# A hybrid decoder layer: low halves of the values in the ones' columns, and the probabilities added up on GpSimd

## The chip, the cores and the metric
The kernel runs on one core of a Trainium2 chip. The metric is the device time of one execution in microseconds. The core has a matrix engine (TensorE, PE in the profile), VectorE (DVE), ScalarE (ACT), GpSimd (POOL) and SyncE (SP), which issues nearly all DMAs. Each engine works through its own queue in order; semaphores join them.

## The reference
One layer of a decoder on x of 2048 tokens by 1024. After a normalisation, one projection feeds three token mixers side by side: a gated linear recurrence, forgetting attention with 6 heads of 64, and gated linear attention with 4 heads. Their outputs pass one projection and a residual, then a gated feed-forward layer of width 2816. The change is inside the forgetting attention, cut here to what matters:

```python
s = (jnp.einsum('bhqd,bhkd->bhqk', qb, k) * scale
     + cb[..., :, None] - cum[..., None, :])
s = jnp.where(k_pos[None, :] <= q_pos[:, None], s, -jnp.inf)
p = jax.nn.softmax(s, axis=-1)
return jnp.einsum('bhqk,bhkd->bhqd', p, v)
```

## The kernel before
All is float32. Matrix products are made of float32r operands: each value is split into a high half (a copy in float32r) and a low half (value minus high half), and a product is three: high x high, high x low, low x high (`split_products`, L77 to L79). The first function, `project_in_and_recur`, projects three of the four blocks of 512 tokens. The second, `mix_and_feed_forward`, projects the last block and runs everything else.

The second function is a row of 328 units on TensorE. A unit is one output tile of 128 x 512: 8 triples of products (6 in some), weights of 128 x 1024. Its kinds are p (projection), o (output projection), g and u (gate and up), d (down). For each unit SyncE loads the raw weights, ScalarE makes the high half `w_hi` (L1108), GpSimd the low half `w_lo` (L1093) as soon as the unit two before is done on TensorE, and VectorE reads the result out of PSUM.

The token mixers are woven into these units: `side` gives for each unit a list of turns, and TensorE does them between the triples of the unit, evenly spaced. All engines walk through the same list in the same order. Attention of block b is woven into units 14 to 22 (block 0), 61 to 89, 139 to 165 and 215 to 241. Its steps are, by letter:

- S: a piece of the scores, 128 queries by up to 512 keys (L1665, L1666; with the mask L1668), into one of two banks of `fa_s_ps`. VectorE takes its row maxima (L1383, `fa_ch_max`). A piece needs its bank free: `bank_free` waits for the reader of the use before the last.
- M: VectorE joins the maxima and splits them (L1388, cast L1393, L1395, `fa_m_cols`), TensorE turns them (L1675), ScalarE copies them into rows of the queries (L1146). The first T of the head waits for it.
- T: scores again, transposed, 128 keys by up to 512 queries, less the maximum (L1691, L1692). ScalarE makes of them `fa_probs` (exponentials in float32, L1141) and `fa_p_hi` (the same in float32r, L1142), VectorE the low half `fa_p_lo` (L1401). There are three buffers of each.
- V: the products with the values (`times_v`, L1707 to L1709) into `fa_o_ps`, two turns after the T of the same item. Values are loaded as 192 columns per key tile: high halves, ones, low halves.
- F: the end of a head (`finish`), issued in the turn of the second key tile of the next head.

An item is one head and one tile of 128 keys. A head of block b has 4(b+1) items; the last three have 384, 256 and 128 query columns, all others 512. Over 4 blocks and 6 heads that is 240 items and 24 heads. In a turn of block 1 to 3 stand one T, one V and one or two S; a unit carries 2 turns in block 1, 2 to 3 in block 2, 3 to 4 in block 3, and 3 in block 0.

Before, the three products of an item are these: high halves and ones (128 columns) times `p_hi`, low halves (64 columns) times `p_hi` into partitions 0 to 63, high halves and ones times `p_lo`. So partitions 0 to 63 of `fa_o_ps` hold the sum of probabilities times values and partitions 64 to 127 the sum of the probabilities, 64 times. `finish` is a reciprocal of the latter (L1408) and a product (L1412).

GpSimd runs, for each unit, the split of the weights, and now and then memsets: `value_ones(b)` (L1048) fills the ones into `fp_v_nat` at the head of each block's operand stage.

Of the kernel before, what the change touches and what calls it, by code (L numbers as in the profile page):

```python
# [14 lines left out]
F32 = mybir.dt.float32  # L15
F32R = mybir.dt.float32r
U32 = mybir.dt.uint32
ALU = mybir.AluOpType
# [538 lines left out]
def mix_and_feed_forward(nc, vec, mod, held, xT, w_in, w_gates, w_alpha, w_out, w_gate_up, w_down, consts, fox_rows, proj, mix, q_split, ka, kb, v_split, yT):  # L557
# [136 lines left out]
    bank_uses = lambda s: [s] if s[0] in ("S", "M", "mean") else [("gate0", s[1]), ("gate1", s[1])] if s[0] == "L" else {("X", 1): [("rows", s[1][0])], ("G", 0): [("z", s[1][:2])], ("G", 4): [("att0", s[1][:2]), ("att1", s[1][:2])],  # L694
# [46 lines left out]
    with ExitStack() as ctx:  # L741
# [20 lines left out]
        mean_ones, eps, scale_a = sb("ff_mean_ones", [P, P]), sb("ff_eps", [P, 1]), sb("ff_scale_a", [P, KD])  # L762
        ident, ident_r, masks_r = sb("fa_ident", [P, P]), sb("fa_ident_r", [P, P], F32R), sb("fa_masks_r", [P, 2, P], F32R)
# [8 lines left out]
        with region:  # L772
# [4 lines left out]
            v_nat = there("fp_v_nat", [P, 2, 2, TPB, 3 * HEAD_DIM], F32R)  # L777
# [9 lines left out]
        with region:  # L787
# [7 lines left out]
            inv_sum, o_t = there("fa_inv_sum", [HEAD_DIM, BLK]), there("fa_o_t", [P, 2, BLK])  # L795
# [7 lines left out]
        v_hi, v_ones, v_lo = (v_nat[:, :, :, :, i * HEAD_DIM:(i + 1) * HEAD_DIM] for i in range(3))  # L803
# [21 lines left out]
        m_turned, m_copied = sem("fa_m_turned"), sem("fa_m_copied")  # L825
        st_done, p_hi_done, p_lo_done, pv_done, inv_done, fin_done = sem("fa_st_done"), sem("fa_p_hi_done"), sem("fa_p_lo_done"), sem("fa_pv_done"), sem("fa_inv_done"), sem("fa_fin_done")
# [5 lines left out]
        v_t, v_hi_done, v_lo_done, ones_made = sem("fp_v_t"), sem("fp_v_hi_done"), sem("fp_v_lo_done"), sem("fp_ones_made")  # L832
# [45 lines left out]
        with nc.Block() as block:  # L878
# [156 lines left out]
            def _(pool):  # L1035
# [38 lines left out]
                def prepare(j):  # L1074
                    for b in range(NBLK):
                        if j >= GIVEN and j in (x_load[b], g_load[b], q_fill[b], fill_at[b]):
                            pool.wait_ge(lo_ready, split(j))
                        if j == x_load[b]:
                            value_ones(b)
# [867 lines left out]
```

## Time and profile before

| | |
|---|---|
| median of 3 runs | 2987.01 us (2985.84 to 2988.37) |
| the profiled execution | 2993.32 us, its span 2991.5 us |
| granted TensorE clock, mean | 0.973 |
| TensorE matmul busy | 2818.5 us, 94% of the span, 12416 instructions |
| VectorE busy | 1463.1 us, 49% |
| ScalarE busy | 1185.2 us, 40% |
| GpSimd busy | 1035.5 us, 35%, 488 instructions |
| DMA queue q1, share of 16 engines | 44.6% |

Busy time is the union of an engine's instructions. Matmuls overlap each other in the records (a record holds the time through the array as well), so what a matmul costs in a stream is read from one start to the next. In the rows below a name such as L1708 is a line of the kernel, and an entry in brackets behind an instruction is the time its engine stood idle before it, and what it waited for.

### The profile page before, as it was taken

The page shows a single profiled execution, that of the slowest core. Times are in us where ns is not written, and L with a number is a line of the kernel's source. Part 1 is how long each engine was busy: PE and PEld are TensorE (multiplying, and loading weights), DVE is VectorE, ACT ScalarE, POOL GpSimd, SP SyncE. Part 2 cuts the span into 40 slices and gives each one's busy share as a digit, 9 for nine tenths or more (in the row PEclk, how much of TensorE's full clock was granted, in tenths as well). Part 3 has the DMA queues.
Part 4 walks back from the last instruction along what each step waited for, and adds up shares of the span by engine and source line. Part 5 has one row for each costly group of instructions (what it writes and reads, how often), then busy time and mean ns, then how long its engine had stood idle before and what let it go on. Part 6 is the DMA issues. An engine that isn't in the chain of part 4 may idle for free.

```text
span 2991.5 us, 32965 instructions
## 1 busy us (share of the span) xinstructions
PE 2818.5 (94%) x12416; PEld 2211.5 (74%) x12416; DVE 1463.1 (49%) x1876; ACT 1185.2 (40%) x1654; POOL 1035.5 (35%) x488
## 2 busy tenths in 40 slices
PE   8998998788988999999999999999999999999999
PEld 4786876466757777886777777867777777778887
DVE  3968786466564334435443454463435554421111
ACT  3333333343345244444433545454335455332222
POOL 2545453221324332243333222334332112444443
PEclk9999999789999999999999999999999999999999
DMA  7555535525644344444624454545245553423233
GB/s 266 180 167 178 166 130 162 171 78 159 220 123 138 105 134 130 130 152 145 184 74 126 140 150 123 161 149 173 74 130 150 151 150 114 144 98 96 94 99 92
DMA packets 159902, 419.05 MB, mean 140 GB/s; under 512 B 18284, under 2 KB 20604, under 8 KB 156672
## 3 DMA queue, kind: packets, MB, share of 16 engines
q1 hardware_dynamic: 157408, 412.48, 44.6%
q10 hardware_dynamic: 2336, 4.46, 0.4%
q8 instruction: 99, 1.62, 0.2%
q14 instruction: 59, 0.48, 0.1%
HBM read 355.95 MB, written 60.92 MB: 139 GB/s over the span
## 4 chain that ended last, share of the span: by engine, by line
PE 64%; DVE 7%; ACT 4%; issue 3%; DMA 3%; SPq 2%; POOL 1%; ACTq 0%; POOLq 0%; DVEq 0%
PE ff_acc_ps L77 17%; PE ff_acc_ps L78 16%; PE ff_acc_ps L79 16%; DMA ff_w_raw<-in_w_gate_up 2%; PE fa_st_ps L1691 1%; PE fa_o_ps L1707 1%; PE fa_s_ps L1665 1%; PE fa_st_ps L1692 1%; PE fa_o_ps L1709 1%; PE fa_o_ps L1708 1%; PE fa_s_ps L1666 1%; DVE ff_silu L1371 1%; DVE fa_inv_sum L1408 1%; SPq L956 1%; PE fa_o_ps L1781 1%
## 5 line engine op out<-in xcount | busy, mean ns | idle before, releaser
L1093 POOL TENSOR_TENSOR w_lo<-ff_w_raw,w_hi 128x1024 fp32r<-128x1024 f32 (+1 forms) x326 | 771.9, 2368 | 1626.7 <-PE ff_acc_ps L79 1553.7
L77 PE MATMUL ff_acc_ps<-h_odd_hi,w_hi 128*128 128x512 f32 x1856 | 752.2, 405 | 50.7 <-DVE h_odd_lo L1376 13.4
L78 PE MATMUL ff_acc_ps<-h_odd_lo,w_hi 128*128 128x512 f32 x1856 | 738.3, 398 | 0.0
L79 PE MATMUL ff_acc_ps<-h_odd_hi,w_lo 128*128 128x512 f32 x1856 | 736.7, 397 | 0.0
L1108 ACT ACTIVATE w_hi<-ff_w_raw 128x1024 fp32r<-128x1024 f32 (+1 forms) x326 | 338.7, 1039 | 935.8 <-PE ff_acc_ps L79 721.5
L77 PEld LDWEIGHTS ff_acc_ps<-h_odd_hi,w_hi 128*128 128x128 f32 x1856 | 357.2, 192 | 160.2 <-issue 63.6
L79 PEld LDWEIGHTS ff_acc_ps<-h_odd_hi,w_lo 128*128 128x128 f32 x1856 | 356.7, 192 | 78.4
L78 PEld LDWEIGHTS ff_acc_ps<-h_odd_lo,w_hi 128*128 128x128 f32 x1856 | 358.2, 193 | 72.7 <-issue 1.7
L77 PE MATMUL ff_acc_ps<-ff_a_hi,w_hi 128*128 128x512 f32 x704 | 285.2, 405 | 10.1 <-issue 6.1
L1401 DVE TENSOR_TENSOR fa_p_lo<-fa_probs,fa_p_hi 128x512 fp32r<-128x512 f32 x240 | 154.4, 644 | 286.7 <-ACT fa_p_hi L1142 286.4
L78 PE MATMUL ff_acc_ps<-ff_a_lo,w_hi 128*128 128x512 f32 x704 | 280.2, 398 | 0.0
L79 PE MATMUL ff_acc_ps<-ff_a_hi,w_lo 128*128 128x512 f32 x704 | 279.9, 398 | 0.0
L211 POOL TENSOR_TENSOR w_lo<-w_raw,w_hi 128x1024 fp32r<-128x1024 f32 x74 | 183.1, 2475 | 219.4 <-PE g_ps L79 163.2
L1141 ACT ACTIVATE fa_probs<-fa_st_ps 128x512 f32<-128x512 f32 x240 | 128.3, 535 | 230.3 <-PE fa_st_ps L1692 151.7
L1383 DVE TENSOR_REDUCE fa_ch_max<-fa_s_ps 128x1 f32<-128x512 f32 (+1 forms) x240 | 144.6, 607 | 137.9 <-PE fa_s_ps L1666 80.5
L1575 DVE TENSOR_TENSOR ff_gated<-ff_silu,ff_acc_ps 128x512 f32<-128x512 f32 x88 | 60.4, 687 | 309.0 <-PE ff_acc_ps L79 272.2
L250 ACT ACTIVATE w_hi<-w_raw 128x1024 fp32r<-128x1024 f32 x74 | 78.4, 1059 | 281.2 <-DMA w_raw<-in_w_in 254.2
L1577 DVE TENSOR_TENSOR ff_a_lo<-ff_gated,ff_a_hi 128x512 fp32r<-128x512 f32 x88 | 110.2, 1252 | 121.3 <-ACT ff_a_hi L1287 121.3
L77 PEld LDWEIGHTS ff_acc_ps<-ff_a_hi,w_hi 128*128 128x128 f32 x704 | 133.1, 189 | 46.4 <-issue 14.8
L77 PE MATMUL g_ps<-h_even_hi,w_hi 128*128 128x512 f32 x384 | 158.0, 411 | 9.8 <-POOL w_lo L211 5.6
L79 PEld LDWEIGHTS ff_acc_ps<-ff_a_hi,w_lo 128*128 128x128 f32 x704 | 133.4, 189 | 32.3
L78 PEld LDWEIGHTS ff_acc_ps<-ff_a_lo,w_hi 128*128 128x128 f32 x704 | 133.3, 189 | 32.0 <-issue 1.7
(263 smaller groups left out, 4047.5 us busy)
## 6 DMA issues: line engine op xcount, KB each, us to landing
ff_w_raw<-in_w_gate_up SPq DMA_DIRECT2D x176, 512.0 KB, 4.1
w_raw<-in_w_in SPq DMA_DIRECT2D x74, 512.0 KB, 4.3
ff_w_raw<-in_w_down SPq DMA_DIRECT2D x64, 512.0 KB, 3.6
mod_w<-in_w_mod SPq DMA_DIRECT2D x24, 1024.0 KB, 5.5
fa_v<-v_split_dram SPq DMA_DIRECT2D x60, 384.0 KB
ff_w_raw<-in_w_out SPq DMA_DIRECT2D x32, 512.0 KB, 3.9
fa_ks_a<-ka_dram SPq DMA_DIRECT2D x60, 256.0 KB
fa_kt_a<-ka_dram SPq DMA_DIRECT2D x60, 256.0 KB
```

Source lines behind the costliest of these rows:

```text
L77: nc.tensor.matmul(out, hi, act_hi, start=first, stop=False)
L78: nc.tensor.matmul(out, hi, act_lo, start=False, stop=False)
L79: return nc.tensor.matmul(out, lo, act_hi, start=False, stop=last)
L211: nc.gpsimd.tensor_tensor(w_lo[:, j % LO], w_raw[:, j % RAW], w_hi[:, j % HI].bitcast(F32), ALU.subtract).then_inc(lo_ready, 1)
L250: nc.scalar.activation(w_hi[:, j % HI], w_raw[:, j % RAW], ACT.Copy).then_inc(hi_ready, 1)
L1093: nc.gpsimd.tensor_tensor(w_lo[:, j % LO, wide], w_raw[:, j % RAW, wide], w_hi[:, j % HI, wide].bitcast(F32), ALU.subtract).then_inc(lo_re ...
L1108: nc.scalar.activation(w_hi[:, j % HI, wide], w_raw[:, j % RAW, wide], ACT.Copy).then_inc(hi_ready, 1)
L1141: nc.scalar.activation(probs[:, m % PB, r * P:], st_ps[:, m % 2, r * P:], ACT.Exp)
L1383: nc.vector.tensor_reduce(ch_max[:, U % 2, i, c:c + 1], s_ps[:, bank_of(("S", n)), 0:w], AX.X, ALU.max).then_inc(max_done, 1)
L1401: nc.vector.tensor_tensor(p_lo[:, m % PB, r * P:], probs[:, m % PB, r * P:], p_hi[:, m % PB, r * P:].bitcast(F32), ALU.subtract).then_inc( ...
L1575: nc.vector.tensor_tensor(gated[:, i % 2], silu[:, i % 2], acc, ALU.mult).then_inc(gated_ready, 1)
L1577: nc.vector.tensor_tensor(a_lo[:, i % AR], gated[:, i % 2], a_hi[:, i % AR].bitcast(F32), ALU.subtract).then_inc(a_ready, 1)
```

## The change
The values lose their ones' columns: a key tile is now 128 columns, high halves and low halves (`VW` = 128 instead of 192, in SBUF and in memory). An item's products are two: high and low halves times `p_hi`, which puts the high part into partitions 0 to 63 and the low part into partitions 64 to 127, and high halves times `p_lo` into partitions 0 to 63. GpSimd adds up `fa_probs` over the items of a head into `fa_p_sum`, two buffers: a copy for the first item, an addition for each of the others (`add_up`). In GpSimd's queue the additions of a unit's T steps stand behind the weight split of the next unit. ScalarE's exponentials of item m wait for the addition of item m-3. At F, TensorE multiplies `fa_p_sum` with ones of 128 x 64 (`total`, float32) into a bank of `fa_s_ps`, and VectorE copies partitions 64 to 127 of `fa_o_ps` to `fa_o_sum`, adds partitions 0 to 63, takes the reciprocal of the total and multiplies. The memset of the ones per block and ScalarE's wait for it go.

```diff
-    bank_uses = lambda s: [s] if s[0] in ("S", "M", "mean") else ...
+    bank_uses = lambda s: [s] if s[0] in ("S", "M", "mean") else [("tot", s[1])] if s[0] == "F" else ...
...
-            v = there("fa_v", [P, 2, TPB, 3 * HEAD_DIM], F32R)
+            v = there("fa_v", [P, 2, TPB, VW], F32R)
...
+            p_sum = there("fa_p_sum", [P, 2, BLK])
...
-                def value_ones(b):
-                    if b >= 1:
-                        pool.wait_ge(mix_ready, KD * b)
-                    nc.gpsimd.memset(v_ones.rearrange("p w h t d -> p (w h t) d").bitcast(F32), 1.0).then_inc(ones_made, 1)
-                    pool.wait_ge(ones_made, b + 1)
+                nc.gpsimd.memset(sum_ones[:], 1.0).then_inc(made, 1)
+                pool.wait_ge(made, 5)
+                def add_up(m):
+                    U, kt = ITEMS[m]
+                    r = max(0, kt - TPB * HEADS[U][0])
+                    pool.wait_ge(p_hi_done, m + 1)
+                    if kt == 0:
+                        if U >= 2:
+                            pool.wait_ge(tot_done, U - 1)
+                        nc.gpsimd.tensor_copy(p_sum[:, U % 2], probs[:, m % PB]).then_inc(sum_done, 1)
+                    else:
+                        pool.wait_ge(sum_done, m)
+                        nc.gpsimd.tensor_tensor(p_sum[:, U % 2, r * P:], p_sum[:, U % 2, r * P:], probs[:, m % PB, r * P:], ALU.add).then_inc(sum_done, 1)
...
                     prepare(j)
+                    if j >= 1:
+                        for kind, n in steps_of(j - 1):
+                            if kind == "T":
+                                add_up(n)
...
                     if m >= PB:
                         act.wait_ge(pv_done, m - PB + 1)
+                        act.wait_ge(sum_done, m - PB + 1)
...
-                        act.wait_ge(ones_made, b + 1)
...
-                    nc.vector.reciprocal(inv_sum[:], o_ps[HEAD_DIM:P, U % 2]).then_inc(inv_done, 1)
+                    nc.vector.tensor_copy(o_sum[:], o_ps[HEAD_DIM:P, U % 2]).then_inc(o_added, 1)
+                    dve.wait_ge(o_added, 2 * U + 1)
+                    nc.vector.tensor_tensor(o_sum[:], o_ps[0:HEAD_DIM, U % 2], o_sum[:], ALU.add).then_inc(o_added, 1)
+                    dve.wait_ge(tot_done, U + 1)
+                    nc.vector.reciprocal(inv_sum[:], s_ps[0:HEAD_DIM, bank_of(("tot", U))]).then_inc(inv_done, 1)
...
-                    nc.vector.tensor_tensor(o_t[...], o_ps[0:HEAD_DIM, U % 2], inv_sum[:], ALU.mult).then_inc(fin_done, 1)
+                    nc.vector.tensor_tensor(o_t[...], o_sum[:], inv_sum[:], ALU.mult).then_inc(fin_done, 1)
...
-                    nc.tensor.matmul(o_ps[:, U % 2, qs], v[:, x % 2, t, 0:VW], p_hi[:, m % PB, qs], start=first, stop=False, ...)
-                    nc.tensor.matmul(o_ps[0:HEAD_DIM, U % 2, qs], v[:, x % 2, t, VW:], p_hi[:, m % PB, qs], start=False, stop=False, ...)
-                    nc.tensor.matmul(o_ps[:, U % 2, qs], v[:, x % 2, t, 0:VW], p_lo[:, m % PB, qs], start=False, stop=end, ...).then_inc(pv_done, 1)
+                    nc.tensor.matmul(o_ps[:, U % 2, qs], v[:, x % 2, t], p_hi[:, m % PB, qs], start=first, stop=False, ...)
+                    nc.tensor.matmul(o_ps[0:HEAD_DIM, U % 2, qs], v[:, x % 2, t, 0:HEAD_DIM], p_lo[:, m % PB, qs], start=False, stop=end, ...).then_inc(pv_done, 1)
+                def total(U):
+                    pe.wait_ge(sum_done, last_item(U) + 1)
+                    pe.wait_ge(made, 5)
+                    bank_free(("tot", U))
+                    nc.tensor.matmul(s_ps[0:HEAD_DIM, bank_of(("tot", U))], sum_ones[:], p_sum[:, U % 2], start=True, stop=True).then_inc(tot_done, 1)
```

## Rows read from the trace of the kernel before

**Rows 1.** Engines' busy time in the last attention stretch, block 3.
```profile
core 0: us, PE busy (x) PEld busy (x) DVE busy (x) ACT busy (x) POOL busy (x), PEclk, DMA share, GB/s
2180.00:2530.00 350.00, 335.85 (x1519) 268.10 (x1518) 177.97 (x255) 169.58 (x273) 79.30 (x34) 0.99 0.48 139
```

**Rows 2.** Who waited for whom, and who waited for L1383: us, times.
```profile
PE fa_s_ps L1675 <- DVE fa_m_cols L1395: 17.8, 14, 2.2
PE fa_s_ps L1665 <- DVE fa_ch_max L1383: 13.6, 11, 5.0
PE fa_o_ps L1707 <- DVE fa_p_lo L1401: 0.3, 1, 0.3
...
  PEld fa_s_ps L1665: 17.7, 14
```

**Rows 3.** Records of L1708, then TensorE's timeline in block 3: start, us.
```profile
L1708 PE MATMUL fa_o_ps<-fa_p_hi,fa_v x240: 222/392/403, 696.8 to 2525.2; 128*64 128x512 f32 x96, 128*64 128x256 f32 x24
...
2302.62 0.40 PE L1707 MATMUL fa_o_ps<-fa_p_hi,fa_v 128*128 128x512 f32 x1
...
2303.32 0.39 PE L77 MATMUL ff_acc_ps<-h_odd_hi,w_hi 128*128 128x512 f32 x1
...
2328.29 0.28 PE L1708 MATMUL fa_o_ps<-fa_p_hi,fa_v 128*64 128x256 f32 x1
2328.41 0.28 PE L1709 MATMUL fa_o_ps<-fa_p_lo,fa_v 128*128 128x256 f32 x1
...
2330.46 0.23 PE L1708 MATMUL fa_o_ps<-fa_p_hi,fa_v 128*64 128x128 f32 x1
2330.52 0.27 PE L1709 MATMUL fa_o_ps<-fa_p_lo,fa_v 128*128 128x128 f32 x1
```

**Rows 4.** TensorE's timeline around a product in float32.
```profile
2170.17 0.39 PE L79 MATMUL ff_acc_ps<-h_odd_hi,w_lo 128*128 128x512 f32 x1
...
2170.40 1.02 PE L1789 MATMUL fa_s_ps<-ga_one_e,ga_head_ones 128*128 128x512 f32 x2
...
2171.49 0.40 PE L78 MATMUL ff_acc_ps<-h_odd_lo,w_hi 128*128 128x512 f32 x1
```

**Rows 5.** GpSimd's instructions by shape: count, busy us, mean ns.
```profile
L222 POOL TENSOR_TENSOR ssum<-ssum,sq 128x512 f32<-128x512 f32 x28 | 36.7, 1309 | 34.7 <-ACT sq L256 31.5 <-POOL ssum L222 0.5
...
L1048 POOL MEMSET fp_v_nat<- 128x1024 f32 x4 | 3.8, 958 | 8.8 <-DVE h_odd_lo L1361 8.6
...
L220 POOL COPY ssum<-sq 128x512 f32<-128x512 f32 x4 | 3.0, 762 | 16.6 <-ACT sq L256 16.6
```

**Rows 6.** Timeline in block 3: two engines released by one matmul; the next split.
```profile
2304.90 0.69 DVE L1575 TENSOR_TENSOR ff_gated<-ff_silu,ff_acc_ps 128x512 f32<-128x512 f32 x1 [0.27 <-PE ff_acc_ps L79]
...
2305.01 2.41 POOL L1093 TENSOR_TENSOR w_lo<-ff_w_raw,w_hi 128x1024 fp32r<-128x1024 f32 x1 [10.77 <-PE ff_acc_ps L79]
...
2315.76 2.40 POOL L1093 TENSOR_TENSOR w_lo<-ff_w_raw,w_hi 128x1024 fp32r<-128x1024 f32 x1 [8.35 <-PE ff_acc_ps L79]
```

**Rows 7.** VectorE's instructions at a head's end, and a copy out of PSUM.
```profile
L1408 DVE RECIPROCAL fa_inv_sum<-fa_o_ps 64x512 f32<-64x512 f32 x24 | 80.6, 3359 | 10.6 <-PE fa_o_ps L1709 9.9
...
L1412 DVE TENSOR_TENSOR fa_o_t<-fa_o_ps,fa_inv_sum 64x512 f32<-64x512 f32 x24 | 16.4, 683 | 0.8
...
L1329 DVE COPY ff_gated<-ff_acc_ps 128x512 f32<-128x512 f32 x10 | 6.9, 691 | 9.4 <-PE ff_acc_ps L79 9.3
```

**Rows 8.** Timeline of a maximum's chain with GpSimd busy.
```profile
2373.67 2.36 POOL L1093 TENSOR_TENSOR w_lo<-ff_w_raw,w_hi 128x1024 fp32r<-128x1024 f32 x1 [9.55 <-PE ff_acc_ps L79]
...
2374.42 1.64 DVE L1393 CAST fa_m_cols<-fa_neg_max 128x4 fp32r<-128x4 f32 x1
...
2376.41 0.44 PE L1675 MATMUL fa_s_ps<-fa_ident_r,fa_m_cols 128*68 128x128 f32 x4 [2.18 <-DVE fa_m_cols L1395]
```

**Rows 9.** Timeline of a maximum's chain with GpSimd idle.
```profile
1674.24 0.42 DVE L1401 TENSOR_TENSOR fa_p_lo<-fa_probs,fa_p_hi 128x256 fp32r<-128x256 f32 x1 [2.46 <-ACT fa_p_hi L1142]
...
1674.78 0.17 DVE L1393 CAST fa_m_cols<-fa_neg_max 128x4 fp32r<-128x4 f32 x1
1674.98 0.17 DVE L1395 TENSOR_TENSOR fa_m_cols<-fa_neg_max,fa_m_cols 128x4 fp32r<-128x4 f32 x1
```

More of the change, by code:

```diff
@@ L693, in mix_and_feed_forward @@
     after.update({at["d", b, HALF_KD, 2]: [("mean", b + 1)] for b in range(NBLK - 1)})
-    bank_uses = lambda s: [s] if s[0] in ("S", "M", "mean") else [("gate0", s[1]), ("gate1", s[1])] if s[0] == "L" else {("X", 1): [("rows", s[1][0])], ("G", 0): [("z", s[1][:2])], ("G", 4): [("att0", s[1][:2]), ("att1", s[1][:2])],
+    bank_uses = lambda s: [s] if s[0] in ("S", "M", "mean") else [("tot", s[1])] if s[0] == "F" else [("gate0", s[1]), ("gate1", s[1])] if s[0] == "L" else {("X", 1): [("rows", s[1][0])], ("G", 0): [("z", s[1][:2])], ("G", 4): [("att0", s[1][:2]), ("att1", s[1][:2])],
                                                                   ("G", 7): [("gmean", s[1][:2])]}.get((s[0], s[1][-1]), []) if s[0] in ("X", "G") else []
@@ L762, in mix_and_feed_forward @@
         mean_ones, eps, scale_a = sb("ff_mean_ones", [P, P]), sb("ff_eps", [P, 1]), sb("ff_scale_a", [P, KD])
+        sum_ones = sb("fa_sum_ones", [P, HEAD_DIM])
         ident, ident_r, masks_r = sb("fa_ident", [P, P]), sb("fa_ident_r", [P, P], F32R), sb("fa_masks_r", [P, 2, P], F32R)
@@ L776, in mix_and_feed_forward @@
             qk_hi, qk_lo = there("fp_hi", [P, 2, BLK], F32R), there("fp_lo", [P, 2, BLK], F32R)
-            v_nat = there("fp_v_nat", [P, 2, 2, TPB, 3 * HEAD_DIM], F32R)
+            v_nat = there("fp_v_nat", [P, 2, 2, TPB, VW], F32R)
         region = ExitStack()
@@ L802, in mix_and_feed_forward @@
         ones_row = ones_col[FF_ROW:FF_ROW + FOX_HEADS].to_broadcast([FOX_HEADS, BLK])
-        v_hi, v_ones, v_lo = (v_nat[:, :, :, :, i * HEAD_DIM:(i + 1) * HEAD_DIM] for i in range(3))
+        v_hi, v_lo = (v_nat[:, :, :, :, i * HEAD_DIM:(i + 1) * HEAD_DIM] for i in range(2))
         k_end, k_dec, q_dec, squares, g_rstd = z, grow, e_neg, one_e, b_cum
@@ L1075, in prepare @@
                     for b in range(NBLK):
-                        if j >= GIVEN and j in (x_load[b], g_load[b], q_fill[b], fill_at[b]):
+                        if j >= GIVEN and j in (g_load[b], q_fill[b], fill_at[b]):
                             pool.wait_ge(lo_ready, split(j))
-                        if j == x_load[b]:
-                            value_ones(b)
                         if j == g_load[b]:
@@ L1641, in bank_free @@
                         pe.wait_ge(att_masked, 2 * (GLA_T * n[0] + n[1]) + int(kind[-1]) + 1)
+                    if kind == "tot":
+                        pe.wait_ge(inv_done, n + 1)
                     if kind in ("gate0", "gate1"):
@@ L1706, in times_v @@
                     qs, first, end, t = slice(r * P, BLK), kt == 0, kt == TPB * b + TPB - 1, kt % TPB
-                    nc.tensor.matmul(o_ps[:, U % 2, qs], v[:, x % 2, t, 0:VW], p_hi[:, m % PB, qs], start=first, stop=False, skip_group_check=True)
-                    nc.tensor.matmul(o_ps[0:HEAD_DIM, U % 2, qs], v[:, x % 2, t, VW:], p_hi[:, m % PB, qs], start=False, stop=False, skip_group_check=True)
-                    nc.tensor.matmul(o_ps[:, U % 2, qs], v[:, x % 2, t, 0:VW], p_lo[:, m % PB, qs], start=False, stop=end, skip_group_check=True).then_inc(pv_done, 1)
+                    nc.tensor.matmul(o_ps[:, U % 2, qs], v[:, x % 2, t], p_hi[:, m % PB, qs], start=first, stop=False, skip_group_check=True)
+                    nc.tensor.matmul(o_ps[0:HEAD_DIM, U % 2, qs], v[:, x % 2, t, 0:HEAD_DIM], p_lo[:, m % PB, qs], start=False, stop=end, skip_group_check=True).then_inc(pv_done, 1)
+                def total(U):
[3 more added lines that the diff above has]
+                    nc.tensor.matmul(s_ps[0:HEAD_DIM, bank_of(("tot", U))], sum_ones[:], p_sum[:, U % 2], start=True, stop=True).then_inc(tot_done, 1)
                 def turn_values(b, t):
@@ L1815, in attend @@
                             times_v(n)
+                        if kind == "F":
+                            total(n)
                 for j in range(N):
```

10 lines of the change are left out of this document (6 added, 4 removed).

## The prediction

> **What bounds the kernel now.** I read the page's busy shares first, then the stretches in which heads are attended, then who waited for whom. In the last attention stretch TensorE is busy 335.85 of 350 us at a granted clock of 0.99 (the 2.4 GHz level), VectorE 178, ScalarE 170 and GpSimd 79 [rows 1]. So TensorE's instruction count sets the time, and the 14 us it stands idle there are the second thing to look at. The waits name them: TensorE stood before the turning of the maxima (L1675) for 17.8 us in 14 places, waiting for fa_m_cols, and before a score piece (L1665) for a free bank, 13.6 us counted at the matmul in 11 places and 17.7 us at its weight load in 14 more [rows 2]. These 39 places are where VectorE is already the later one, and where anything that delays VectorE shows at once. Everywhere else a few microseconds of delay have cover.
>
> **TensorE: one product fewer per key tile.** Each of the 240 items loses one of three products, L1708 (240 records [rows 3]). The price of a product is not the 0.39 us of its record, since matmuls are pipelined; it is the distance from start to start. At 512 columns the four starts are 0.70 us apart, 0.233 each; at 256 columns 0.12, at 128 columns 0.06 [rows 3]; for 384 I take 0.18, between 0.233 and 0.12. A head of block b has 4b+1 items at 512 columns and one each at 384, 256 and 128: over 24 heads 168, 24, 24, 24. Removed: 168 x 0.233 + 24 x (0.18 + 0.12 + 0.06) = 39.1 + 8.6 = 47.8 us. It doesn't matter which of the three goes, they are equally far apart.
>
> **TensorE: one float32 product per head.** fa_sum_ones and fa_p_sum are float32, not float32r. The float32 product of L1789 at 512 columns shows what that costs: from the start of the L79 before it to the second ordinary product behind it pass 1.32 us [rows 4], of which two ordinary intervals are 0.46; so 0.86 us. 24 x 0.86 = 20.6 us. Its output is 64 partitions, not 128, which changed nothing for L1708 against its neighbours, so I keep 0.86. Bounds: 0.233 (were it an ordinary product, 5.6 us) and 1.02, the length of its two records together (24.5 us). Net on TensorE: 47.8 - 20.6 = 27.2 us.
>
> **GpSimd: 240 additions.** The nearest rows are the additions of the same shape, 1.31 us for 128x512, and the copy, 0.76 us [rows 5]. 24 copies x 0.76 + 144 full additions x 1.31 + 24 x 1.31 x (0.75 + 0.5 + 0.25) = 18 + 189 + 47 = 254 us more on GpSimd; four ones' memsets of 0.96 us go. Is it late? Two weight splits in block 3 start 10.75 us apart [rows 6], each taking 2.4 us; with up to four items in a unit GpSimd has 2.4 + 4 x 1.31 = 7.6 us of work in 10.75. Behind an addition in GpSimd's queue stands the split of the next weights. The last addition of a unit can end some 2 us after the unit; the split then starts 1 to 2 us late, and its reader is the unit after the one now starting, some 10 us away; SyncE's next weight load and ScalarE's high half wait behind it with the same cover. ScalarE's new wait (item m for the addition of m-3) asks that the first addition of a unit, behind a split, be done when the fourth item comes: about 2.4 + 1.3 us, up to 6 us with waits for VectorE, against about 8 us (the fourth turn comes three quarters into the 10.75). So this wait costs nothing; without that cover it would hold exponentials, then the low halves, then L1707. Block 0 has three items a unit, three of four narrower, and so less of this work.
>
> **VectorE: the end of a head.** It was a reciprocal of 3.36 and a product of 0.68 us [rows 7]. Added are a copy out of PSUM, at most 0.69 us by the copy of the same length [rows 7], and an addition, 0.68; and the wait for TensorE's total, which is issued behind the V of the same turn and takes under 1.3 us, beside the copy and addition. So the end of a head holds VectorE about 5.5 instead of 4.0 us. Queued behind it are the next piece's maximum and the next low half; L1707 needs that low half two turns later, the bank one to two turns later, and three turns fill about one interval of 10.75 us. Covered, except a little: 1 us in all. The bank that the total takes waits for a maximum already read, since VectorE does it ahead of the end of the head.
>
> **VectorE against GpSimd.** This is the cost I think decides how much is left. A cast of 128x4 values on the way to fa_m_cols took 1.64 us where GpSimd ran a split, and ended with it (2374.42 + 1.64 against 2373.67 + 2.36); TensorE waited 2.18 us [rows 8]. With GpSimd idle the same cast takes 0.17 us [rows 9]. Every item now ends its exponential by releasing two readers at once, VectorE's low half and GpSimd's addition. Released by the same matmul, VectorE starts 0.11 us before GpSimd [rows 6], so the low half mostly goes first and the addition follows. But the chain for the maxima is low half, reduction, cast, subtraction in 0.91 us [rows 9], and the cast now meets the addition of the same item, 256 wide in blocks 1 to 3, about 0.66 us. Between nothing (the addition has ended) and 1.31 + 0.66 us (another is queued), I take 0.5 us in each of the 14 places: 7 us, bounds 0 and 28. At the 25 bank waits the maximum itself reads PSUM, and only a low half ahead of it can be late: 0 to 1.31 us each, 0 to 33 us; I take 4, since the low half usually wins. Where TensorE waits for such a chain anyway, the product removed ahead of it is not gained: at most 39 x 0.233 = 9 us, I take 3.
> The Trainium skill (SBUF — State Buffer, SBUF: two separate sides) says that VectorE, in a two-port mode or with two SBUF inputs, and GpSimd take a shared pair of ports as an exclusive lock, for the whole instruction. The cast that ended with the split agrees, and it speaks against this change; the rival that it makes is the last but one below.
>
> **Off the path.** The loads of fa_v shrink by a third, the two memory layouts with them; the one wait of L1707 in the whole table is 0.3 us for a low half [rows 2], none for a load, so I count nothing, and keep 3 us of gain as the bound (earlier key loads in the same queue). The ones' memsets and their semaphore go from the head of the operand stage; their reader ScalarE waits there for TensorE's transposes anyway.
>
> **Sum.** -47.8 + 20.6 + 7 + 4 + 3 + 1 = -12.2 us. Against the profiled execution (span 2991.5, 2993.3 us in all) that is 2981.1; that execution stands 6.3 us above the median of 2987.0, so the comparable time is 2974.8, rounded 2975. What a measurement here can tell from no change is 0.2%, 6 us: under 2981 is faster, above 2993 slower.
>
> **Rivals.**
> All the new work is hidden (chance 0.25): only the net on TensorE counts, 2987.0 - 27.2 = 2960. For it: GpSimd has about 3 us to spare in every unit, and L1707 hardly ever waits [rows 2]. Against: the 39 places without slack.
> The forecast, half of it given back (0.40): 2975, between 2966 and 2981.
> The gain is eaten (0.21): 0.68 us more at each of the 39 places is 26.5 us; time 2981 to 2993, centre 2986. For it: two instructions of about that length are now released together each time.
> Slower (0.14): GpSimd takes the ports first, or two additions stand in a row behind a split, so that each of the 39 places pays a full addition: 39 x 1.31 = 51 us, less 27.2, is +24, 3011. It decides from 0.85 us a place (27.2 + 6 over 39). For it: the order of the two engines hangs on 0.11 us, and when VectorE is busy at the release, GpSimd is first. Against: most of the additions end well before the next item, about 3 us later. By the lock that the Trainium skill states (same page and section) each low half and addition exclude one another, whichever comes first.
> That the change doesn't do what it says: the removed product saves less, because the low half is now waited for. One wait for it of 0.3 us is in the trace [rows 2]; I hold it within the third case.
>
> **Numbers.** Faster by over 0.2%: the first two and a little of the third, 0.66. Within 0.2%: 0.20. Slower: 0.14. The range must leave out no more than 2 in 10: 2957 (all hidden and 3 us for shorter loads) to 2994, past the third case. The forecast's own range is 2966 to 2981.
>
> **What would show it.** L1707 and L1709 with 240 records each and no third line; the total 24 times with two records each, about 1.02 us together. TensorE busy some 27 us less. Additions near 1.31 us, longer where VectorE holds them. L1675 waiting for fa_m_cols 7 us more than 17.8, casts of 0.5 us and more where they were 0.17; bank waits up by 4 us. GpSimd's busy time near 1290 us, and no wait of ScalarE for an addition. Wrong would be: additions far over 1.31 us, waits at L1691 or L1707 of more than a few microseconds in total, weight splits that come too late for L77, or a clock that falls because stalls have grown.

## The result, and the profile after

The changed kernel takes 3005.9 us (median of 6 runs, 3000.1 to 3011.1), the kernel before on the same chips 2983.3 (6 runs, 2978.8 to 2988.4). The ratio is 1.0073, 95% interval 1.0059 to 1.0086: some 22 us slower, where 12 us faster was forecast, and above the range of 2957 to 2994. The profiled execution has a span of 3003.7 us; that of the kernel before, 2991.5, came from a run 10 us above the median of these six, so the two traces lie only 12.2 us apart.

The page of the kernel after: its span, and busy time, share and instructions of each engine.

```profile
span 3003.7 us, 33138 instructions
...
PE 2802.9 (93%) x12224; PEld 2171.8 (72%) x12224; DVE 1556.7 (52%) x1924; ACT 1185.7 (39%) x1654; POOL 1369.8 (46%) x725
```

The records are as the change has them: 12416 - 240 + 48 = 12224 matmuls, two for each total. TensorE's busy time went down by 15.6 us, its idle time (span less busy) went up by 27.8, from 173.0 to 200.8. Engines' busy time in the stretch of [rows 1], kernel after:

```profile
core 0: us, PE busy (x) PEld busy (x) DVE busy (x) ACT busy (x) POOL busy (x), PEclk, DMA share, GB/s
2180.00:2530.00 350.00, 325.09 (x1414) 250.52 (x1413) 204.63 (x262) 169.76 (x272) 221.95 (x129) 0.98 0.46 131
```

Against [rows 1] TensorE is idle 24.9 of 350 us, not 14.2; VectorE went from 178 to 205 us, GpSimd from 79 to 222. VectorE's mean instruction grew too (0.70 to 0.78 us), so it does not only have more to do.

Who waited for whom in the kernel after (engine, tile and line, releaser: us, times, longest; PEld is the weight load of the line's matmul):

```profile
PEld fa_s_ps L1686 <- DVE fa_ch_max L1397: 26.2, 20, 5.4
PE fa_s_ps L1696 <- DVE fa_m_cols L1409: 23.9, 17, 2.4
PE fa_s_ps L1686 <- DVE fa_ch_max L1397: 20.5, 17, 5.0
PE fa_o_ps L1728 <- DVE fa_p_lo L1415: 5.0, 5, 2.2
PE fa_s_ps L1686 <- DVE fa_inv_sum L1426: 3.6, 3, 1.6
PE fa_s_ps L1735 <- DVE fa_ch_max L1397: 2.7, 3, 1.6
```

Against [rows 2], at the matmuls: a piece's wait for its bank (now L1686) went from 13.6 to 20.5 us; the turning of the maxima (now L1696) from 17.8 to 23.9; the low half from 0.3 to 5.0; and two are new, for a bank that holds a total until the reciprocal has read it (3.6), and of the total for a bank (2.7). The added waits are 6.9 + 6.1 + 4.7 + 3.6 + 2.7 = 24.0 us of the 27.8. All have VectorE as the releaser. No wait of ScalarE for an addition is in the table of waits.

The PEld row is shown and not added. Where a piece waits for its bank, its weight load and its matmul wait together: the longest load wait, 5.4 us, and the longest matmul wait, 5.0, are at the same piece, and 9 of the 11 matmul waits of before, 13 of the 17 of after, have a load wait that ends with them, to 0.01 us. Adding the two rows would count that time twice.

The time by stage, in us between the starts of ScalarE's high halves of the units at either end of an attention stretch:

| block | before | after | two products alone (e1) |
|---|---|---|---|
| 0 | 106.6 | 121.1 | 107.5 |
| 1 | 240.4 | 239.0 | 231.6 |
| 2 | 271.6 | 272.9 | 260.7 |
| 3 | 313.1 | 320.0 | 298.5 |
| sum | 931.7 | 953.0 | 898.3 |

In these stretches after is 21.3 us longer; outside them its trace is 9.1 us shorter, as the whole spans differ by 12.2. The loss is greatest in block 0, which has six heads' ends but only 24 items, of which 6 at full width. Block 0 alone doesn't say which part costs it: over e1's 107.5 us, e4 below (additions, old end) has 109.6 there, e3 (new end, no additions) 112.2, and both together 121.1. These are single executions, and the granted clock in this stretch is 0.94 in before and in e3, 0.92 in e4, 0.90 in after and in e1.

**The clock.** Over all runs the mean granted clock is lower in the kernel after: 0.9727 (6 runs, 0.971 to 0.974), where the 90 runs of the kernel before that stand beside the experiments have 0.9756. The profiled execution of before happens to be one of its runs at a low clock (0.973). Among those 90, the 22 at 0.974 or less (0.9738 on the mean) took 2989.7 us and the 24 at 0.977 or more (0.9772) 2982.3. By that, as an estimate, 0.0029 goes with 6 of the 22 us; 9 if the whole time went with the clock. Whether the clock is lower because TensorE stands idle more often, no run here separates.

### The profile page after: what moved, and what is told of

Its sections match the earlier page's. It is cut to its first block, busy times and chain, and to the rows that moved or that the text cites. A ratio compares the mean times of both kernels' runs of the same rounds, so it can differ in the third digit from the quotient of the medians.

```text
span 3003.7 us, 33138 instructions
## 1 busy us (share of the span) xinstructions
PE 2802.9 (93%) x12224; PEld 2171.8 (72%) x12224; DVE 1556.7 (52%) x1924; ACT 1185.7 (39%) x1654; POOL 1369.8 (46%) x725
## 4 chain that ended last, share of the span: by engine, by line
PE 60%; DVE 10%; ACT 4%; issue 4%; DMA 2%; SPq 2%; POOL 1%; ACTq 0%; POOLq 0%; DVEq 0%
PE ff_acc_ps L77 16%; PE ff_acc_ps L79 16%; PE ff_acc_ps L78 16%; PE fa_s_ps L1686 1%; DVE fa_inv_sum L1426 1%; PE fa_st_ps L1712 1%; PE fa_s_ps L1687 1%; PE fa_o_ps L1728 1%; PE fa_st_ps L1713 1%; DVE fa_p_lo L1415 1%; PE fa_o_ps L1729 1%; DMA ff_w_raw<-in_w_gate_up 1%; DVE ff_silu L1385 1%; DVE ff_a_lo L1596 1%; SPq L959 1%
## 5 line engine op out<-in xcount | busy, mean ns | idle before, releaser
L1061 POOL TENSOR_TENSOR fa_p_sum<-fa_p_sum,fa_probs 128x512 f32<-128x512 f32 (+3 forms) x216 | 310.5, 1438 | 265.4 <-ACT fa_p_hi L1157 260.2
L1415 DVE TENSOR_TENSOR fa_p_lo<-fa_probs,fa_p_hi 128x512 fp32r<-128x512 f32 x240 | 195.1, 817 | 252.1 <-ACT fa_p_hi L1157 251.2
L1596 DVE TENSOR_TENSOR ff_a_lo<-ff_gated,ff_a_hi 128x512 fp32r<-128x512 f32 x88 | 119.2, 1355 | 118.0 <-ACT ff_a_hi L1301 118.0
```

The costliest lines, as they stand in the source:

```text
L1061: nc.gpsimd.tensor_tensor(p_sum[:, U % 2, r * P:], p_sum[:, U % 2, r * P:], probs[:, m % PB, r * P:], ALU.add).then_inc(sum_done, 1)
L1415: nc.vector.tensor_tensor(p_lo[:, m % PB, r * P:], probs[:, m % PB, r * P:], p_hi[:, m % PB, r * P:].bitcast(F32), ALU.subtract).then_inc( ...
L1596: nc.vector.tensor_tensor(a_lo[:, i % AR], gated[:, i % 2], a_hi[:, i % AR].bitcast(F32), ALU.subtract).then_inc(a_ready, 1)
```

## The experiments

Each kernel was timed in turns with the kernel before on the same chip. Ratios carry 95% intervals; "us" is the ratio times 2985, less 2985. Differences of two such values are good to 6 to 12 us; the width is given where it matters. Diffs are shortened and are against the kernel after, if not said otherwise. Waits and timelines come from one profiled execution of each kernel.

### The change taken apart: e1 to e4

Two theories stood here. Theory A: the additions cost the time, by holding up VectorE. Theory B: the end of a head, with its total, costs it, and the additions are covered.

e1: two products alone; no additions, no total, VectorE's old end of a head.

```diff
-  add_up(n)                                  # GpSimd, and ScalarE's wait for sum_done
-  total(n)                                   # TensorE
-  tensor_copy(o_sum, o_ps[HEAD_DIM:P]); tensor_tensor(o_sum, o_ps[0:HEAD_DIM], o_sum, ALU.add)
-  nc.vector.reciprocal(inv_sum[:], s_ps[0:HEAD_DIM, bank_of(("tot", U))])
+  nc.vector.reciprocal(inv_sum[:], o_ps[0:HEAD_DIM, U % 2])
```

> The two products alone, with the narrower values: no additions, no total, the end of a head as before (its reciprocal reads partitions 0 to 63 of fa_o_ps, so the output is not the attention's). What is left is the saving on TensorE. Both theories expect the 47.8 us of the prediction less what TensorE gives back in waiting: 40 to 48 us under before (ratio 0.984 to 0.987). Should the removed product have been covered, it would be under 25 us.

Measured: 0.9864 (0.9841 to 0.9886), -41 us.

e2: the kernel before with GpSimd's additions (and ScalarE's wait for them), their sum used by nobody.

```diff
   prepare(j)
+  for kind, n in steps_of(j - 1):            # in the kernel before
+      if kind == "T": add_up(n)
+  act.wait_ge(sum_done, m - PB + 1)
```

> The kernel before with the 240 additions on GpSimd and ScalarE's wait for them, and nothing that reads the sum. Theory A (the additions hold VectorE's low halves and casts, and so TensorE): 30 to 45 us over before (ratio 1.010 to 1.015). Theory B (the end of a head, with its total, is what costs; the additions are covered): under 10 us.

Measured: 1.0036 (1.0020 to 1.0053), +11 us.

e3: two products, the total and the new end of a head; instead of the additions one memset a head.

```diff
-  nc.gpsimd.tensor_copy(p_sum[:, U % 2], probs[:, m % PB]); ... tensor_tensor(..., ALU.add)
+  nc.gpsimd.memset(p_sum[:, U % 2], 1.0)     # first item of a head only
```

> The changed kernel without its 216 additions; in place of the copy at a head's first item stands a memset of the same buffer to 1, so the total is not the sum of the probabilities. Two products, total and the new end of a head stay. Theory A: 15 to 24 us under before (about 47 saved, 24 for the totals, up to 8 for the end of a head; ratio 0.992 to 0.995). Theory B: 5 to 15 us over before.

Measured: 0.9995 (0.9981 to 1.0009), -1.5 us.

e4: two products and the additions; no total, the old end of a head.

> The changed kernel with two products and the additions, without the total and with the end of a head as before (its reciprocal reads partitions 0 to 63 of fa_o_ps, so the output is not the attention's). Theory A: 0 to 12 us under before, since the additions take about 40 of the 47. Theory B: 35 to 45 us under before.

Measured: 0.9944 (0.9924 to 0.9964), -17 us.

The four make a square with the kernel after, all on two products:

| | old end of a head | total and new end |
|---|---|---|
| no additions | e1 -41 | e3 -1.5 |
| GpSimd's additions | e4 -17 | after +22 |

The additions cost 24 us in the left column and 23 in the right; the end of a head costs 39 us in the upper row and 39 in the lower. The parts add up: -41 + 24 + 39 = +22. Within the intervals (each of these four differences is good to 6 to 9 us) no interplay of the two made the kernel slower, and the larger of the two costs is the one that I had put at 20.6 + 1. Neither theory holds alone: e3 and e4 lie between what A and B expected, and e2 is just above B's 10 us.

TensorE's busy and idle time (span less busy) in the profiled executions show where each part goes:

| | span | PE busy | PE idle | granted clock, mean of all runs |
|---|---|---|---|---|
| before | 2991.5 | 2818.5 | 173.0 | 0.9756 |
| e1 | 2952.1 | 2772.6 | 179.5 | 0.9755 |
| e3 | 2977.6 | 2793.9 | 183.7 | 0.9751 |
| e4 | 2973.5 | 2777.5 | 196.0 | 0.9734 |
| after | 3003.7 | 2802.9 | 200.8 | 0.9727 |

The additions add to the idle time (16.5 and 17.1 us) and go with a lower clock; the end of a head adds above all to the busy time (21.3 and 25.4), which is its float32 product, and 4 to 5 us of idle time. (The profiled execution of e1 is 10 us above its median.)

### The end of a head: f1, f4, g4, h1, k1

f1: the total in float32r, one pass.

```diff
-  sum_ones = sb("fa_sum_ones", [P, HEAD_DIM])          p_sum = there("fa_p_sum", [P, 2, BLK])
+  sum_ones = sb("fa_sum_ones", [P, HEAD_DIM], F32R)    p_sum = there("fa_p_sum", [P, 2, BLK], F32R)
```

> The changed kernel with fa_p_sum and fa_sum_ones in float32r, so that the total is one ordinary product (the sum is rounded at each addition). If the end of a head costs by its product on TensorE: each falls from about 1.0 us to 0.23, so 24 x 0.75 = 18 us less than the changed kernel, near 1.001 of before. If it costs by what waits for VectorE and the bank: under 8 us less.

Measured: 1.0040 (1.0026 to 1.0054), +12 us, so 10 less than after (±6); the two cases expected 18 and under 8.

TensorE's timeline at a total, kernel after (start, length; x2 is its two records):

```profile
2396.17 0.40 PE L1729 MATMUL fa_o_ps<-fa_p_lo,fa_v 128*64 128x512 f32 x1
2396.50 1.07 PE L1735 MATMUL fa_s_ps<-fa_p_sum,fa_sum_ones 128*64 128x512 f32 x2
2397.50 0.50 PE L77 MATMUL ff_acc_ps<-ff_a_hi,w_hi 128*128 128x512 f32 x1
2397.83 0.39 PE L78 MATMUL ff_acc_ps<-ff_a_lo,w_hi 128*128 128x512 f32 x1
```

Read as the prediction read [rows 4]: from the product ahead to the second one behind 1.66 us, less two ordinary intervals of 0.23, is 1.20 us, where the row of before gave 0.86. Of the 24 totals 20 give 1.14 to 1.21, one 1.28, and three that stood in a wait more. So by the timeline the term is 28.8 us, not 20.6. In float32r it would be 5.6, a saving of 23; 10 came. The two traces show where the rest went: from after to f1 TensorE's busy time fell by 20.0 us (2802.9 to 2782.9) and its idle time rose by 12.2 (200.8 to 213.0). f1's table of waits has, for a bank held by a total and for the low half,

```profile
PE fa_s_ps L1686 <- DVE fa_inv_sum L1426: 8.6, 6, 2.6
PE fa_o_ps L1728 <- DVE fa_p_lo L1415: 8.2, 7, 3.1
```

5.0 and 3.2 us above after's. TensorE arrives earlier where VectorE is the later one.

f4: the kernel after without VectorE's copy and addition.

```diff
-  nc.vector.tensor_copy(o_sum[:], o_ps[HEAD_DIM:P, U % 2])
-  nc.vector.tensor_tensor(o_sum[:], o_ps[0:HEAD_DIM, U % 2], o_sum[:], ALU.add)
-  nc.vector.tensor_tensor(o_t[...], o_sum[:], inv_sum[:], ALU.mult)
+  nc.vector.tensor_tensor(o_t[...], o_ps[0:HEAD_DIM, U % 2], inv_sum[:], ALU.mult)
```

> The changed kernel with the total, but without VectorE's copy and addition at a head's end: the product reads partitions 0 to 63 of fa_o_ps, the low part in 64 to 127 is left out. If VectorE's 1.4 us more per head are what is paid: 10 to 15 us less than the changed kernel. If they are covered: within 4 us of it.

Measured: 1.0011 (0.9993 to 1.0029), +3 us: 19 less than after (±7), more than the 10 to 15 of the first case. Two instructions of 0.69 and 0.68 us, 24 times, are 33 us of VectorE's time at an engine busy for half of the span. In the two traces TensorE's idle time fell from 200.8 to 185.8 us.

g4: e1 with the copy and the addition, nothing on GpSimd, no total.

```diff
   # against e1
+  nc.vector.tensor_copy(o_sum[:], o_ps[HEAD_DIM:P, U % 2])
+  nc.vector.tensor_tensor(o_sum[:], o_ps[0:HEAD_DIM, U % 2], o_sum[:], ALU.add)
   nc.vector.reciprocal(inv_sum[:], o_ps[0:HEAD_DIM, U % 2])
-  nc.vector.tensor_tensor(o_t[...], o_ps[0:HEAD_DIM, U % 2], inv_sum[:], ALU.mult)
+  nc.vector.tensor_tensor(o_t[...], o_sum[:], inv_sum[:], ALU.mult)
```

> Two products, no additions, no total, but VectorE's copy, addition and the product from SBUF at a head's end (the reciprocal reads partitions 0 to 63 of fa_o_ps). It shows what f4 took away with GpSimd at rest. If VectorE's 1.4 us a head are paid by their length: 12 to 18 us over e1 (ratio 0.990 to 0.9925). If they cost only where additions of GpSimd block them: within 5 us of e1's 0.9864.

Measured: 0.9954 (0.9939 to 0.9969), -14 us: 27 more than e1 (±8), with GpSimd at its weight splits alone, where 12 to 18 was the larger expectation. And the total, put on top of it, costs only 12 more (e3 over g4, ±6), though it takes 28.8 us of TensorE: in e3's trace the pieces' matmuls wait 16.0 us for their banks, in g4's 26.3, so while TensorE is in the total, VectorE catches up. So the two costs of a head's end overlap, and 39 us is the price of both, not to be split cleanly. The timeline of VectorE and TensorE at a head's end in g4:

```profile
2317.63 0.69 DVE L1415 COPY fa_o_sum<-fa_o_ps 64x512 f32<-64x512 f32 x1
2318.36 0.68 DVE L1417 TENSOR_TENSOR fa_o_sum<-fa_o_ps,fa_o_sum 64x512 f32<-64x512 f32 x1
2318.96 3.34 DVE L1418 RECIPROCAL fa_inv_sum<-fa_o_ps 64x512 f32<-64x512 f32 x1
2320.95 0.39 PE L1678 MATMUL fa_s_ps<-fa_ks_a,fa_q_a 128*128 128x512 f32 x1
2322.34 0.69 DVE L1423 TENSOR_TENSOR fa_o_t<-fa_o_sum,fa_inv_sum 64x512 f32<-64x512 f32 x1
...
2323.72 0.68 DVE L1390 TENSOR_REDUCE fa_ch_max<-fa_s_ps 128x1 f32<-128x512 f32 x1
2324.46 0.50 PE L1678 MATMUL fa_s_ps<-fa_ks_a,fa_q_a 128*128 128x512 f32 x1 [1.25 <-DVE fa_ch_max L1390]
```

One piece of the scores was issued at 2318.14 (not shown), the next at 2320.95, into the other bank, while VectorE is in the reciprocal. The maximum of the first comes only at 2323.72, when the end of the head has run out, and the piece after them, at 2324.46, needs that first bank: the matrix engine stands idle for 1.25 us. The pieces go through two banks. A hold of VectorE of 5.4 us instead of 4.1 uses them up here; at the same place in e1 (pieces at 2310.26, 2313.07 and 2315.16) the first maximum starts at 2314.39, and the matmul of the third piece shows no wait. The bank's waits in e1 and in g4, lines of the two tables of waits:

```profile
PEld fa_s_ps L1674 <- DVE fa_ch_max L1390: 23.2, 20, 5.4
PE fa_s_ps L1674 <- DVE fa_ch_max L1390: 17.6, 14, 5.0
```

```profile
PEld fa_s_ps L1678 <- DVE fa_ch_max L1390: 35.7, 29, 5.4
PE fa_s_ps L1678 <- DVE fa_ch_max L1390: 26.3, 21, 5.0
```

At the matmuls 17.6 us in 14 places became 26.3 in 21, 8.7 more (the load rows are the same waits again, for the most part). TensorE's idle time rose by 15.7 us in all, from 179.5 to 195.2; 3.4 of the rest is L1720's wait for the low half. The traces lie 16.4 us apart and not 27. The mean clock of all runs is 0.9755 for e1 and 0.9722 for g4, which by the estimate above goes with some 7 us. So about a third of the 27 us is seen at the banks.

h1: the kernel after with the end of a head in two turns: copy and addition in the turn of the first key tile of the next head, total, reciprocal and product one turn later, as before.

```diff
+  if kt == 0 and U > first: turn.append(("E", U - 1))      # E: copy and addition
```

> The changed kernel, with VectorE's copy and addition of a head's end one turn earlier (the turn of the next head's first item), so that a low half and a maximum stand between them and the reciprocal; the amount of work is unchanged. If the unbroken 5.4 us on VectorE at a head's end are what TensorE pays: 8 to 18 us less than the changed kernel (ratio 1.001 to 1.005). If it is the amount of VectorE's work, wherever it stands: within 4 us of 1.0073.

Measured: 1.0053 (1.0036 to 1.0070), +16 us; 6 less than after (±6), between the two cases.

k1: g4 with the same split.

> g4 (two products, no additions on GpSimd, no total, VectorE's copy and addition at a head's end), with the copy and addition one turn earlier, as in h1. If the unbroken stretch on VectorE is the cost: within 6 us of e1 (ratio 0.986 to 0.989). If it is the amount of VectorE's work near a head's end: g4's 0.995, within 6 us.

Measured: 0.9910 (0.9879 to 0.9942), -27 us, between e1 and g4: 13 less than g4 (±10). Its bank waits:

```profile
PEld fa_s_ps L1684 <- DVE fa_ch_max L1392: 24.4, 25, 5.4
PE fa_s_ps L1684 <- DVE fa_ch_max L1392: 16.9, 14, 5.0
```

At the matmuls 16.9 us, e1's 17.6 again, though VectorE does the same instructions as in g4. So g4's added waits at the banks come from the unbroken stretch and not from the amount of work. TensorE's idle time, 189.2 us, is still 9.7 above e1's (2.7 of it before the turned maxima). The time came back only by about half, which is neither of the two cases; where the other half goes is open.

### The additions: f5, f2, g1

f5: e4, but GpSimd writes zeros for as long as it would add (nothing is read).

```diff
-  nc.gpsimd.tensor_tensor(p_sum[...], p_sum[...], probs[...], ALU.add)
+  nc.gpsimd.memset(p_sum[:, 0:356 * (TPB - r)], 0.0)
```

> As e4 (two products, end of a head as before), but in place of each addition GpSimd writes a memset of about the same length, which reads nothing; released at the same time and waited for by ScalarE in the same way. If the additions cost because GpSimd reads SBUF while VectorE has two inputs there: low halves no longer wait, and the time is near e1's 0.986 (within 6 us). If they cost by GpSimd's queue (late splits of the weights, ScalarE's wait): near e4's 0.994.

Measured: 0.9876 (0.9847 to 0.9905), -37 us, as expected if the reading is the cost. The same queue and the same waits, the length of an addition that nothing holds up (1.29 us; e4's take 1.68), and of the 24 us of the additions 20 are gone (±11). Groups by shape, f5 and then e4 (count | busy us, mean ns | idle before):

```profile
L1060 POOL MEMSET fa_p_sum<- 128x1424 f32 x144 | 185.5, 1288 | 186.8 <-ACT fa_p_hi L1156 184.6
...
L1414 DVE TENSOR_TENSOR fa_p_lo<-fa_probs,fa_p_hi 128x512 fp32r<-128x512 f32 x168 | 126.0, 750 | 193.5 <-ACT fa_p_hi L1156 193.3
```

```profile
L1413 DVE TENSOR_TENSOR fa_p_lo<-fa_probs,fa_p_hi 128x512 fp32r<-128x512 f32 x168 | 154.9, 924 | 177.8 <-ACT fa_p_hi L1155 177.3
```

Beside the memsets a low half of 512 columns takes 750 ns, as in e1 (745); beside additions 924. It is the reading of GpSimd, or what it does to VectorE's reading, that costs, and not how late GpSimd's queue runs; a queue later by the 0.39 us an addition that the memsets lack was not tried by itself. The Trainium skill (SBUF — State Buffer, SBUF: two separate sides) says that VectorE with two inputs in SBUF is held up by GpSimd where GpSimd reads SBUF; f5 and e4 agree.

f2: in the kernel after an addition waits for VectorE's low half of its item, so that the low half is always first.

```diff
-  pool.wait_ge(p_hi_done, m + 1)
+  pool.wait_ge(p_lo_done, m + 1)
```

> The changed kernel, but each addition waits for VectorE's low half of the same item, so the low half of an item never waits for its own addition. If the order of the two decides what the additions cost (60 low halves waited behind an addition): 10 to 20 us less than the changed kernel. If only the total time for which GpSimd holds the ports matters: within 4 us of the changed kernel, and the casts are then late more often.

Measured: 1.0056 (1.0034 to 1.0078), +17 us, 5 less than after, not to be told from it. The low half's mean fell (854 ns) and an addition took 1.31 us instead of 1.69, the length that the prediction had from [rows 5]. But the cast on the way to the maxima, which now meets the addition more often, grew from 691 to 827 ns, and L1696 waited 28.0 us instead of 23.9. Order moves the collision, it doesn't remove it.

g1: the additions on VectorE, right behind the low half.

```diff
-  add_up(n)        # GpSimd, behind prepare(j)
+  add_up(n)        # VectorE, in the turn of T, behind prob_low(n)
```

> The changed kernel with the same copies and additions on VectorE, each behind the low half of its item; GpSimd has none. VectorE gets about 240 x 0.6 = 150 us more of its own work but nothing blocks it. If the blocking behind GpSimd (1.3 to 1.7 us an addition) is the cost: 5 to 15 us less than the changed kernel (ratio 1.002 to 1.006). If any time that VectorE loses ahead of the maxima is paid in the same way: the changed kernel's 1.007 or more.

Measured: 1.0105 (1.0089 to 1.0122), +31 us, 10 more than after. From the groups of g1:

```profile
L1410 DVE TENSOR_TENSOR fa_p_sum<-fa_p_sum,fa_probs 128x512 f32<-128x512 f32 x144 | 109.3, 759 | 0.0
...
L1399 DVE TENSOR_TENSOR fa_p_lo<-fa_probs,fa_p_hi 128x512 fp32r<-128x512 f32 x168 | 119.4, 711 | 160.7 <-ACT fa_p_hi L1141 160.2
```

Each is shorter (759 ns, and the low half 711), but all stand in VectorE's queue. So time that VectorE loses ahead of the maxima is paid whatever takes it. GpSimd is the better place, and still costs 23 us.

### Toward a better version: g2, g5, h2, h3

g5: f1, and ScalarE makes the copy of the end of a head. g2: the same with f2's order.

```diff
-  nc.vector.tensor_copy(o_sum[:], o_ps[HEAD_DIM:P, U % 2])
+  nc.scalar.activation(o_sum[:], o_ps[HEAD_DIM:P, U % 2], ACT.Copy)
```

> As g2, but the additions released together with the low halves, as in the changed kernel. Expected 1.000 to 1.002, 0.001 to 0.002 over g2 if f2's order helps here too; within 0.001 of g2 if it does not.

> The changed kernel with the total in float32r, the additions behind VectorE's low halves, and the copy at a head's end on ScalarE in place of VectorE. Adding what f1 (-0.33%), f2 (-0.17%) and half of f4 (-0.3%) gave: ratio 0.999 to 1.000. If the three remove the same waits, it stays at 1.002 or more.

Measured: g5 1.0017 (1.0001 to 1.0033), +5 us; g2 1.0010 (1.0000 to 1.0020), +3 us. They are within 0.001 of each other, so f2's order gives nothing here either.

h2: f1, f2 and the split end of h1. h3: f1, the split end, and the copy on ScalarE.

> h1 with the total in float32r and the additions behind VectorE's low halves. If the split gives what f4 gave and adds to f1 and f2: ratio 0.996 to 0.999, faster than the kernel before. If not: 1.001 or more, as g2.

> The total in float32r, the end split, and the copy in it on ScalarE, the additions released as in the changed kernel. If VectorE's time counts more than the order of the additions: ratio 0.995 to 0.998, 0.001 under h2. If ScalarE's copy delays exponentials: over h2.

Measured: h2 1.0016 (1.0004 to 1.0028), +5 us; h3 0.9987 (0.9972 to 1.0002), -4 us. The split adds nothing to g2 (h2), and h3 falls just short of its 0.995 to 0.998. h3 is the best of those that do all of the work: 0.86% below the kernel after, and not to be told from the kernel before. None is clearly faster than the kernel before.

## Why the prediction was wrong

**What bounds the kernel: "these 39 places".** The reading of [rows 2] counted waits twice. At the matmuls there are 11 waits for a bank and 14 for the maxima, 25 places; the 14 waits of the weight load are mostly the same as those 11 (9 of them stand at the same matmuls). So TensorE stood 31.4 us there, not 49.1; the term priced at "25 bank waits" had 11 of them, and the rivals priced at 39 places had 25.

**TensorE: one product fewer, -47.8, and 3 not gained.** Two products alone gave 41. Right: TensorE's busy time fell by 45.9 us in e1, and its idle time rose by 6.5 (at the banks 4.0, before the turned maxima 1.9). So 6.5 us of the product's time were met by waits, where the prediction had 3 and a bound of 9.

**TensorE: one float32 product, 20.6.** Mis-sized: 1.20 us each by after's timeline, 28.8 us in all, above the bound of 24.5. The bound was the length of the two records, and it did not hold, since the product ahead and the one behind also take 0.1 us more to the next start (0.33 where 0.23 is usual).

**VectorE: the end of a head, "Covered, except a little: 1 us in all".** This is the step that failed most. By itself it costs 27 us (g4 over e1) and, taken out of the kernel after, gives back 19 (f4). The length was nearly right: 5.4 us of hold in g4 and 5.6 in after, medians, against 5.5 predicted (the mean in after is 6.2, the longest 11.9). The cover was not. The prediction counted three turns to an interval of 10.75 us and a low half that is needed two turns later, and called the bank needed one to two turns later covered as well. But the banks are among the places that it had named as without slack: at 4.1 us of hold some of them are exhausted already, and a longer hold adds to the waits there (13.6 us before, 17.6 in e1, 26.3 in g4). That there "anything that delays VectorE shows at once" stood in its first paragraph and was not applied to its own 33 us. With the total the two make 39 us (e3 over e1, after over e4), where 21.6 stood.

**VectorE against GpSimd, 7 + 4.** Right in mechanism, too small: the additions cost 23 to 24 us on two products, and 11 on three (e2). That TensorE's third product covers the difference is argued, not shown. Of 24 casts of 128x4, 17 now take over 0.3 us, 7 before; the median went from 0.17 to 0.50 us, 0.33 more where 0.5 was assumed. What the prediction left out is the low half: the mean at 512 columns went from 745 to 924 ns (e1, e4), 30 us of VectorE's time ahead of the maxima. It reckoned that "the low half mostly goes first", from one item at a time. When VectorE is behind, additions stand in a row and the low halves wait; the timeline of after:

```profile
2509.41 5.20 POOL L1061 TENSOR_TENSOR fa_p_sum<-fa_p_sum,fa_probs 128x512 f32<-128x512 f32 x3 [3.46 <-ACT fa_p_hi L1157]
...
2510.34 3.12 DVE L1415 TENSOR_TENSOR fa_p_lo<-fa_probs,fa_p_hi 128x512 fp32r<-128x512 f32 x2 [0.28 <-ACT fa_p_hi L1157]
```

Three additions in 5.20 us, and two low halves in 3.12 instead of 1.38. That was the rival "slower" in kind, not in size: it asked 1.31 us at every one of 39 places, 51 us, and 23 came; the rest of the slowing is the ends of heads, which it did not have.

**GpSimd: 240 additions, 254 us, hidden.** Its queue cost little: f5, with GpSimd busy for 1285 us and released in the same way, costs 4 us over e1 (±11), and in after ScalarE never stood for an addition. The length was low. The groups of after by shape:

```profile
L1061 POOL TENSOR_TENSOR fa_p_sum<-fa_p_sum,fa_probs 128x512 f32<-128x512 f32 x144 | 243.4, 1690 | 162.6 <-ACT fa_p_hi L1157 159.4
...
L1058 POOL COPY fa_p_sum<-fa_probs 128x512 f32<-128x512 f32 x24 | 24.6, 1024 | 48.6 <-ACT fa_p_hi L1157 48.6
```

1.69 us against the 1.31 of [rows 5], the copy 1.02 against 0.76. With the low half always first (f2) an addition takes 1.31: GpSimd is held up by VectorE's low halves as well. GpSimd's busy time is 1369.8 us, not 1290.

**The signs that the prediction named.** "Additions far over 1.31 us" and "waits at L1691 or L1707 of more than a few microseconds": the second, now L1728, came to 5.0 us, the additions to 1.69, so both spoke. TensorE's busy time fell by 15.6 us, not 27: the totals weighed more. The maxima's wait rose by 6.1 (7 predicted), which was right; the bank waits at the matmuls by 6.9, not 4, and by 6.3 more with the totals' own. The clock did fall, over all runs, from 0.9756 to 0.9727, some 6 to 9 of the 22 us by the estimate above; within the square it goes with the additions (0.9755 to 0.9734, 0.9751 to 0.9727), so it is inside their 24 us and not beside them.

**The sum, measured.** -41 + 24 + 39 = +22, against -44.8 + 11 + 21.6 = -12.2. Of the 34 us between them 17 are the end of a head with its total, 13 the additions, 4 the product's removal; each part is good to 6 to 9 us.

**Left open.** How much of the end's cost is the unbroken stretch and how much VectorE's time: the bank waits say the first (k1), but they hold only a third of it, and the time says half of each, with wide intervals. Why f1 gives only 10 of 23 us is read from one pair of traces and not shown by an experiment of its own. Why the clock is lower is open. Whether a third bank for the score pieces would cover the longer hold was not tried.

## What to carry to other kernels

Where the bounding engine already waits for another at some places, every microsecond added to that other engine's queue is to be priced at these places first, however low its busy share: here 33 us of VectorE at 49% busy cost 19 to 27. Count those places by the matmuls' waits alone; a load's wait beside it is the same time. Work taken off TensorE to "idle" GpSimd was paid here by VectorE, since it reads SBUF while VectorE does; replace it once by memsets of like length, and the two costs (queue, reading) come apart. One trace is one execution: compare the clock over all runs. A change with several parts is best priced as a square of its parts before it is built whole.

## What the runs showed of the hardware

A float32 product of 512 columns costs 1.20 us in a stream of products at 0.23 with weights of 64 columns (20 of 24 places 1.14 to 1.21), and 0.86 in the one stream of the kernel before ([rows 4]; 7 of its 8 places). The weight loads differ. In after:

```profile
2396.50 0.19 PEld L1735 LDWEIGHTS fa_s_ps<-fa_p_sum,fa_sum_ones 128*64 128x64 f32 x2 [0.41 <-issue]
2397.50 0.19 PEld L77 LDWEIGHTS ff_acc_ps<-ff_a_hi,w_hi 128*128 128x128 f32 x1 [0.81 <-issue]
```

In before:

```profile
2170.18 0.41 PEld L1789 LDWEIGHTS fa_s_ps<-ga_one_e,ga_head_ones 128*128 128x128 f32 x2
2170.83 0.19 PEld L77 LDWEIGHTS ff_acc_ps<-h_odd_hi,w_hi 128*128 128x128 f32 x1 [0.24 <-issue]
```

In before the float32 product's weights are loaded 0.22 us ahead of its matmul, with no idle time; in after the load starts with the matmul, 0.41 us of idle time before it, and the next load stands idle for 0.81 us where it is 0.24 in before. What makes the loads late isn't known. A matmul with a weight of 64 columns is no cheaper, start to start, than one with 128 ([rows 3]; f1's totals, 0.23 us).

VectorE's subtraction of two SBUF tiles of 512 columns takes 0.69 us (the median in every kernel here), on the mean 710 to 745 ns where GpSimd has only its weight splits (g4, e1), 750 beside memsets of 1.29 us (f5), and 924 beside additions (e4); GpSimd's own addition goes from 1.31 to 1.69 us.
